# Rotary embedding of a two-block network: the exchange of feature pairs by transfers inside SBUF instead of products on TensorE

## The reference

```python
def apply_rope(x, cos, sin):
    ...
    a, b, c_, d = jnp.split(x, 4, axis=-1)
    rot = jnp.concatenate([-b, a, -d, c_], -1)
    return (x * cos + rot * sin).astype(x.dtype)
```

## Time and profile before

| | us |
|---|---|
| median of three runs | 1642.85 |
| lowest, highest | 1642.05, 1642.93 |
| span of the profiled execution (first to last instruction) | 1641.9 |
| TensorE busy in it | 1581.9 (96%) |
| VectorE busy | 828.0 (50%) |
| ScalarE busy | 735.2 (45%) |
| GpSimd busy | 0.9 |

### The profile page before, as it was taken

The page is one execution under the profiler, slowest core; times in us unless marked ns, Lnnn a source line. Parts: engine busy times, 40 slices in busy tenths (PEclk is TensorE's granted clock), DMA queues, the critical chain, the costliest instruction groups (busy, mean ns, idle before and its releaser), DMA issues.

```text
span 1641.9 us, 27059 instructions
## 1 busy us (share of the span) xinstructions
PE 1581.9 (96%) x11296; PEld 1223.5 (75%) x11296; DVE 828.0 (50%) x1461; ACT 735.2 (45%) x1140; POOL 0.9 (0%) x5
## 2 busy tenths in 40 slices
PE   8999989999999999999989999999999999999987
PEld 5646567777787778789858999998988788535443
DVE  2536664644434444543575756665677675212223
ACT  3545552633212332443463744546545542554444
POOL 0000000000000000000000000000000000000000
PEclk9999999999999999999999999999999999999999
DMA  9412632244334442422212446452442237799995
GB/s 390 157 39 82 212 118 103 103 181 178 124 120 154 166 162 96 180 77 103 78 36 94 158 151 218 148 174 107 163 143 99 82 131 314 298 407 420 421 421 205
DMA packets 43133, 287.91 MB, mean 175 GB/s; under 512 B 4848, under 2 KB 6000, under 8 KB 12160
## 3 DMA queue, kind: packets, MB, share of 16 engines
q1 hardware_dynamic: 42832, 285.99, 46.4%
q10 hardware_dynamic: 144, 0.06, 0.0%
q0 software_dynamic: 32, 0.07, 0.0%
HBM read 285.05 MB, written 1.05 MB: 174 GB/s over the span
## 4 chain that ended last, share of the span: by engine, by line
PE 82%; DVE 7%; ACT 5%; DMA 4%; issue 1%; SPq 0%; DVEq 0%; ACTq 0%
PE ps L539 17%; PE ps L541 16%; PE ps L540 16%; PE ps L2966 7%; DMA deep<-wts 4%; PE ps L590 2%; DVE WL L524 2%; PE ps L2826 1%; PE ps L1569 1%; PE ps L1540 1%; PE ps L1471 1%; PE ps L708 1%; PE ps L1648 1%; PE ps L1647 1%; PE ps L1646 1%
## 5 line engine op out<-in xcount | busy, mean ns | idle before, releaser
L539 PE MATMUL ps<-HH,WH 128*128 128x512 f32 (+2 forms) x1424 | 470.9, 331 | 10.1 <-DVE WL L524 5.7
L541 PE MATMUL ps<-HH,WL 128*128 128x512 f32 (+2 forms) x1424 | 459.9, 323 | 0.0
L540 PE MATMUL ps<-HL,WH 128*128 128x512 f32 (+2 forms) x1424 | 459.4, 323 | 0.0
L524 DVE TENSOR_TENSOR WL<-ring,WH 128x2048 fp32r<-128x2048 f32 (+2 forms) x134 | 281.5, 2103 | 143.5 <-ACT WH L514 143.4
L539 PEld LDWEIGHTS ps<-HH,WH 128*128 128x128 f32 x1424 | 270.0, 190 | 54.7 <-issue 22.5
L514 ACT ACTIVATE WH<-ring 128x2048 fp32r<-128x2048 f32 (+2 forms) x134 | 236.0, 1763 | 153.2 <-PE ps L541 76.6
L541 PEld LDWEIGHTS ps<-HH,WL 128*128 128x128 f32 x1424 | 270.0, 190 | 20.4
L540 PEld LDWEIGHTS ps<-HL,WH 128*128 128x128 f32 x1424 | 270.4, 190 | 18.4
L2966 PE MATMUL ps<-deep,arena 128*32 128x512 f32 (+1 forms) x872 | 114.4, 593 | 10.7 <-ACT late_x L2952 5.6
L539 PE MATMUL ps<-parts,WH 128*128 128x512 f32 (+1 forms) x352 | 119.9, 341 | 0.0
L540 PE MATMUL ps<-parts,WH 128*128 128x512 f32 (+1 forms) x352 | 118.4, 336 | 0.0
(11 more groups left out here) (401 smaller groups left out, 2185.3 us busy)
## 6 DMA issues: line engine op xcount, KB each, us to landing
ring<-wts SPq DMA_DIRECT2D x138, 1024.0 KB, 4.9
deep<-wts SPq DMA_DIRECT2D x92, 1024.0 KB, 16.3
ring<-wts SPq DMA_DIRECT2D x32, 704.0 KB, 4.0
arena<-wts SPq DMA_DIRECT2D x8, 1024.0 KB, 15.6
ring<-wts SPq DMA_DIRECT2D x4, 672.0 KB, 13.7
X<-xin SPq DMA_DIRECT2D x4, 512.0 KB, 16.5
ahead<-wts SPq DMA_DIRECT2D x2, 1024.0 KB, 8.5
deep<-wts SPq DMA_DIRECT2D x4, 512.0 KB, 20.5
```

The source lines that it names most:

```text
L524: e.tensor_tensor(lo, raw(i), hi.bitcast(F32), ALU.subtract).then_inc(*up("low", i))
L539: e.matmul(o, w[0][:, cols], x[0], start=k == 0, stop=False)
L540: e.matmul(o, w[0][:, cols], x[1], start=False, stop=False)
L541: return e.matmul(o, w[1][:, cols], x[0], start=False, stop=k == nk - 1)
```

## The change

The features of each rotated part are put in another order when the weights are laid out on the host (`paired`): the two features of a pair become neighbours, in rows 2i and 2i+1. Scores are sums over the features, and query and key are permuted alike, so that they stay the same. The sine table takes the sign (`rope_sign`). With that order the exchange of partners is an exchange of neighbouring rows. It is done by two transfers of 64 rows (16 for the 32-feature parts) of 1 KB each, from the tile to the temporary inside SBUF, issued from GpSimd's queue (`pool_rope`); the odd rows go to the even ones, and the even to the odd. GpSimd waits for the copy ("kept") and, from the third rope on, for the end of rope n-2, and then issues both; VectorE waits for both (semaphores `s_turned`, one for each temporary). VectorE's three operations stay; those on 96 rows now take only the 32 rows that turn. All of `pe_rope`'s products and their banks go, and with them the waits of TensorE for the copies (`pe_query_rope`, `pe_window_rope`, `pe_key_rope`, `query_rope`). Some marks are renamed, so that they share semaphores (`vs_tokens` into `vm.window`, `queries` into `keys.queries`, `query_tile` into `key_tile.query`, `vm_tile` into `key_tile.values`).

```diff
+def rope_order(dim):
     q = dim // 4
+    return [b + s * q + i for b in (0, 2 * q) for i in range(q) for s in range(2)]
+def paired(w, dim):
+    return w.reshape(w.shape[0], -1, dim)[:, :, rope_order(dim)].reshape(w.shape)
+def rope_sign(dim):
+    return np.where(np.arange(dim) // (dim // 4) % 2, 1, -1).astype(np.float32)[:, None]
...
     c64, s64 = rope_table(64)
+    c64, s64 = paired_rows(c64), paired_rows(s64 * rope_sign(64))
...
+        s_turned = [sem(f"s_turned{i}") for i in range(2)]
...
-        def pe_rope(e, key, dst, rows, perm):
-            b = bank(e, "rope", *key)
-            e.matmul(ps[0:rows, b, 0:256], C(perm, rows)[0:rows, :], dst[0:rows, 0:256], start=True,
-                     stop=True).then_inc(*up("turned", *key))
-            banks.give(b, "rope.sin", *key)
-
-        def dve_rope(e, key, dst, rows, cos, sin, TMP):
-            tm = TMP[0:rows, len(turned_keys) % 2, 0:256]
-            e.wait_ge(*at("turned", *key))
-            if len(turned_keys) >= 2:
+        def rope_place(rows, TMP):
+            low = 0 if rows == 128 else 64
+            return low, TMP[low:rows, len(turned_keys) % 2, 0:256]
+
+        def pool_rope(e, key, dst, rows, TMP, ready):
+            n = len(turned_keys)
+            low, tm = rope_place(rows, TMP)
+            e.wait_ge(*ready)
+            if n >= 2:
                 e.wait_ge(*at("rope", *turned_keys[-2]))
             turned_keys.append(key)
-            e.tensor_tensor(tm, B("rope", *key)[0:rows, 0:256], C(sin)[0:rows, :],
-                            ALU.mult).then_inc(*up("rope.sin", *key))
+            of = dst[low:rows, 0:256]
+            for x in range(2):
+                e.dma_start(tm[x:rows - low:2], of[1 - x:rows - low:2]).then_inc(s_turned[n % 2], 16)
+
+        def dve_rope(e, key, dst, rows, cos, sin, TMP):
+            n = len(turned_keys)
+            low, tm = rope_place(rows, TMP)
+            turned_keys.append(key)
+            e.wait_ge(s_turned[n % 2], 32 * (n // 2 + 1))
+            e.tensor_tensor(tm, tm, C(sin)[low:rows, :], ALU.mult).then_inc(*up("rope.sin", *key))
...
+        def pool_heads(e):
+            pool_rope(e, ("kept.ks",), KS, 128, TMPA, at("kept.ks"))
+            pool_rope(e, ("kept.kr",), KR, 96, TMPA, at("kept.kr"))
+            for h in range(2):
+                pool_query_rope(e, h)
+            for i in range(len(UNITS)):
+                if i in ROPED_AT:
+                    pool_query_rope(e, ROPED_AT[i])
+                if i in WINDOW_ROPED_AT:
+                    m = WINDOW_ROPED_AT[i]
+                    pool_rope(e, ("kept.qs", m), QS[:, m, :], 128, TMPA, at("kept.qs", m))
+
+        def pool_diff_inputs(e):
+            for name, t in (("kept.kd", Kd), ("kept.qd", Qd)):
+                for h in range(8):
+                    pool_rope(e, (name, h), t[:, h, :], 128, TMPD, at(name, h))
...
                     pe_tiles(e, c, ((128 * m, 128, "kept.kd", h),), m == 1)
-                    for r in ((0, 1), (2, 3), (4, 5), (6,))[h - 4]:
-                        pe_key_rope(e, r)
-            pe_key_rope(e, 7)
...
-                    pe_tiles(e, c, ((128 * m, 128, "kept.qd", h),), m == 1, 256, (lambda: query_rope(6)) if h == 7 else None)
-                    if 0 < h < 7:
-                        query_rope(h - 1)
+                    pe_tiles(e, c, ((128 * m, 128, "kept.qd", h),), m == 1, 256)
...
             pe_diff_turn(e, 0)
-            query_rope(7)
             pe_diff_scores(e, 2)
...
         def pool_program(e):
             e.dma_start(MT[:, :], meta).then_inc(s_m, 16)
+            pool_heads(e)
+            pool_diff_inputs(e)
```

More of the change, by code:

```diff
@@ L79, in rope_table, with paired_rows @@
     return cos.T.astype(np.float32), sin.T.astype(np.float32)
-def rope_perm(dim):
+def rope_order(dim):
     q = dim // 4
[L84 to L89, removed]
+    return [b + s * q + i for b in (0, 2 * q) for i in range(q) for s in range(2)]
+def paired(w, dim):
+    return w.reshape(w.shape[0], -1, dim)[:, :, rope_order(dim)].reshape(w.shape)
+def paired_rows(t):
+    return t[rope_order(len(t))]
+def rope_sign(dim):
+    return np.where(np.arange(dim) // (dim // 4) % 2, 1, -1).astype(np.float32)[:, None]
 def consts():
@@ L120, in consts @@
     c32, s32 = rope_table(32)
+    c32, s32 = paired_rows(c32), paired_rows(s32 * rope_sign(32))
     put("cos96", np.concatenate([np.ones((64, S), np.float32), c32]))
@@ L217, in host_chunk @@
         w = x["ab_w_in"][0][256 * key[1]:256 * key[1] + 256]
-        return pack_k(np.concatenate([w[:, :256], w[:, 768:]], 1))
+        return pack_k(np.concatenate([w[:, :256], w[:, 768:896], paired(w[:, 896:928], 32), paired(w[:, 928:1056], 64),
+                                      w[:, 1056:]], 1))
     if kind == "abq":
-        qs = x["ab_w_in"][0][:, 256:768].reshape(D, 8, 64)[:, QPERM].reshape(D, 512)
+        qs = paired(x["ab_w_in"][0][:, 256:768], 64).reshape(D, 8, 64)[:, QPERM].reshape(D, 512)
         return pack_k(qs[:, 256 * key[1]:256 * key[1] + 256])
     if kind == "qb":
-        return pack_k(x["mla_w_qb"][0][:, 384 * key[1]:384 * key[1] + 384])
+        w = x["mla_w_qb"][0][:, 384 * key[1]:384 * key[1] + 384].reshape(256, 4, 96)
+        turned = paired(w[:, :, 64:].reshape(256, 128), 32).reshape(256, 4, 32)
+        return pack_k(np.concatenate([w[:, :, :64], turned], 2).reshape(256, 384))
     if kind == "kvb":
@@ L239, in host_chunk @@
     if kind == "din":
-        return pack_k(x["diff_w_in"][0][:, 256 * key[1]:256 * key[1] + 256])
+        w = x["diff_w_in"][0][:, 256 * key[1]:256 * key[1] + 256]
+        return pack_k(paired(w, 64) if key[1] < 8 else w)
     if kind == "dout":
@@ L1067, in dve_rope @@
             e.wait_ge(*at("rope.cos", *key))
-            e.tensor_tensor(dst[0:rows, 0:256], dst[0:rows, 0:256], tm, ALU.add).then_inc(*up("rope", *key))
+            e.tensor_tensor(dst[low:rows, 0:256], dst[low:rows, 0:256], tm, ALU.add).then_inc(*up("rope", *key))
         HP = parts(8, 512)
@@ L1155, in pe_inputs @@
             t.then_inc(*up("turned.vs"))
[L1156 to L1160, removed]
+            banks.give(b, "vm.window")
             pe_mod(e, 0, 10)
@@ L1168, in pe_inputs, with pe_tiles @@
             pe_tiles(e, c[1], ((128, 128, "kept.qs", 3),))
-        def pe_tiles(e, c, tiles, ends=True, n=512, halfway=None):
+        def pe_tiles(e, c, tiles, ends=True, n=512):
             w = weights(e, c)
@@ L1254, in act_inputs @@
             e.wait_ge(*at("turned.vs"))
-            e.activation(VS, B("turned.vs").rearrange("p (c m) -> p c m", c=4), ACT.Copy).then_inc(*up("vs_tokens"))
+            e.activation(VS, B("turned.vs").rearrange("p (c m) -> p c m", c=4), ACT.Copy).then_inc(*up("vm.window"))
             act_keep(e, QS[:, 2, :], 128, ("kept.qs", 2), at("tile", "kept.qs", 2))
@@ L1308, in pe_queries @@
         def pe_queries(e, w, i, h):
-            b = bank(e, "queries", h)
+            b = bank(e, "keys.queries", h)
             for k in range(2):
@@ L1312, in pe_queries, with pool_query_rope @@
                              stop=k == 1)
[L1313 to L1318, removed]
+            t.then_inc(*up("key_tile.query", h))
+            banks.give(b, "keys.queries", h)
+        def pool_query_rope(e, h):
+            pool_rope(e, ("qm", h), QM[:, h % 4, :], 96, TMPA, at("keys.queries", h))
         def act_queries(e, h):
-            e.wait_ge(*at("query_tile", h))
-            e.activation(QM[0:96, h % 4, :], B("queries", h)[0:96, :], ACT.Copy).then_inc(*up("queries", h))
+            e.wait_ge(*at("key_tile.query", h))
+            e.activation(QM[0:96, h % 4, :], B("keys.queries", h)[0:96, :], ACT.Copy).then_inc(*up("keys.queries", h))
         def dve_queries(e, h):
@@ L1341, in act_prepare @@
             act_keys(e, h)
-        def pe_window_rope(e, m):
-            e.wait_ge(*at("kept.qs", m))
-            pe_rope(e, ("kept.qs", m), QS[:, m, :], 128, "r128")
+        def pool_heads(e):
[13 more added lines that the diff above has]
+                    pool_rope(e, (name, h), t[:, h, :], 128, TMPD, at(name, h))
         def pe_heads(e):
             w = weights(e, index["kvb", 0])
-            for h in range(2):
-                pe_query_rope(e, h)
             for k in range(4):
@@ L1353, in pe_heads @@
                 e.matmul(ps[:, b, :], KV[:, 128 * k:128 * k + 128], w[:, 256:768], start=True,
-                         stop=True).then_inc(*up("vm_tile", k))
+                         stop=True).then_inc(*up("key_tile.values", k))
                 banks.give(b, "vm", k)
@@ L1374, in act_heads @@
             for k in range(4):
-                e.wait_ge(*at("vm_tile", k))
+                e.wait_ge(*at("key_tile.values", k))
                 e.activation(VM[:, k, :], B("vm", k), ACT.Copy).then_inc(*up("vm", k))
@@ L3334, in build @@
         offs = np.cumsum([0] + [128 * c for _, c in plan])
-        whole_free = {("kvb", 0): ("key_tile", 3), ("qb", 0): ("query_tile", 3), ("qb", 1): ("query_tile", 7),
```

(3 more changed lines are left out.)

22 lines of the change are left out of this document (2 added, 20 removed).

## The result

The changed kernel takes 1647.09 us in the median of 20 runs (1642.36 to 1649.91) against 1643.05 us of the kernel before (20 runs, 1641.98 to 1647.11): a ratio of 1.0023, 95% interval 1.0017 to 1.0030. The forecast was 1634.8, and the time lies outside its range. The profiled execution of the changed kernel took 1649.35 us, 2.3 above its median, with a span of 1647.5; before, the span was 1641.9.

The account below looks back on a forecast made before the run. PE, with 82% of the chain, was taken as the bound, VectorE as the limit at the second block's queries. Gains of 3.7, 3.9 and 0.4 us made 8.0 off 1642.85: 1634.8 us, range 1631.5 to 1644.5.

Parts of the forecast that it names:

- The keys' term: Second block's eight key ropes: all 3.9 us of product time on the chain goes, at every L in the bounds.
- KS, KR and the first two queries: First stretch: transfers here are covered by other work, so 2 x 0.87 us is gained.
- the prediction's own term: First stretch (KS, KR, eight MLA queries, four window queries): 3.7 us gained at L = 4, 4.7 at 3.
- L: Time from the end of ScalarE's copy to the landing of both transfers: between 2.9 and 6.5 us, taken as 4.0.
- The queries of the second block: Eight Qd ropes, where VectorE decides: 0.4 us gained of 3.4 at L = 4, 1.7 gained at L = 3.
- the sum: Whole kernel: gains of 3.7, 3.9 and 0.4 make 8.0 us at L = 4, 10.3 at L = 3.
- the first term: First stretch again: 4.5 us less the loss at query 3; 2.4 us gained was given for L = 5.
- a median landing of more than 5 us: Sign named for the forecast being wrong, read from how long the rope transfers take to land.
- the shares of 0.54 and 0.51: DMA engines half busy at some transfer moments, taken to make an L of less than 3 unlikely.
- Slower: Qd ropes at 805 to 822 us wait on two temporaries if weight loads delay transfers: 1646.4 at L = 6.5; chance 0.14.
- Starved splits: VectorE's splits hold up GpSimd's descriptors, rope 2's pair lands 1.8 us later, some 1 us lost: 1635.8; chance 0.04.
- All back: Nearly all product time returns because transfers land in 3 us or less: 1632.5 us; chance 0.17.

Follow-up runs that it names:

- e1: Changed kernel with SyncE's four loads that replace the query and key weights held until the ropes of query 3 and query 7 end: 1636.69 us.
- e3: Changed kernel with the heads' loads and the two 1 MB loads of the second block held together: 1634.74 us, 1635.82 when run again.
- e4: Changed kernel, loads in place, with 20 idle products on PE ahead of its waits for the ropes of query 3 and query 7: 1642.92 us.
- e6: Kernel before, with only the eight ropes of the second block's keys done by transfers, the others still by products: 1641.65 us.

## Why the prediction was wrong

**What was right.** The page and the chain had the bound right, and the terms came out where nothing disturbed them. The table gives the length of the stretches in the profiles, in us, cut at the first copy of MLA's values, the last product of the heads' turn, the first copy of the second block's values, and the first product that weighs its outputs:

| kernel | up to the values | heads | up to the second block's values | its queries and heads | rest |
|---|---|---|---|---|---|
| before | 97.7 | 136.3 | 512.1 | 119.4 | 776.4 |
| after | 94.6 | 144.2 | 508.0 | 123.2 | 777.5 |
| e1, heads' loads held | 96.2 | 134.9 | 508.0 | 121.5 | 778.3 |
| e3, all held | 94.3 | 134.9 | 508.1 | 116.9 | 779.1 |
| e4, PE kept busy | 96.4 | 139.7 | 508.1 | 119.8 | 778.2 |
| e6, keys alone | 97.2 | 136.2 | 508.0 | 121.0 | 778.4 |

The keys' term (3.9 us) measured 4.0 to 4.1 in every kernel that has the transfers there, and PE is busy 40.00 us of 40 between 700 and 740. KS, KR and the first two queries (1.7 us) lie in the first column, which moves by 1 to 2 us with the arrival of the input; in the profile of the changed kernel 1.35 of its 3.1 us are there before any rope. The heads with their loads held take 1.4 us less, and in both profiles a dip of the clock that the kernel before does not have is in that (0.63 at 112 to 116 in e1; 0.86 and 0.72 at 220 to 228 in e3). From the first of the heads' exponentials to the last, ahead of the dip in e3, it takes 121.3 us (99.5 to 220.8) against 124.2 before (103.0 to 227.2): 2.9 less, and the prediction's own term has 3.0 at L = 3 (4.7 less the 1.7 of the first column). The queries of the second block take up to 2.5 less (1.7 at L = 3).

That the sum, 8.0, lies between the gains of the two runs with the loads held, 8.4 and 7.1, is luck. It was worked out for an L of 4; at the quiet L of 2.6 that is measured below, the prediction's sum is over 10.3 (hence the 1632.5 expected of e3), and these runs stay 2 to 3 us under that. The dips of the clock seen in these profiles are likely a part of it; how large a part, no run shows. (At L = 5 the first term should read 4.5 - 1.8 = 2.7 and not 2.4; nothing hangs on it.) The rest differs by 1 to 3 us among the profiles, for which no run shows a cause in the change.

**Where it failed: one L for all ropes.** The step is "L lies between 2.9 and 6.5. I take ... 4.0". From the end of a copy to the landing of both transfers it took 2.6 us in quiet (rope 0 of Qd: 790.40 to 792.97), below the lower bound, and 5.8, 6.6 and 6.2 at query 3, query 7 and rope 2 (106.42 to 112.18, 146.77 to 153.41, 796.17 to 802.37), once above the upper bound. L had two values and not one, and the larger fell on three ropes that had less room than that: at query 3 the scores start at 113.82, where a quiet L of 2.5 would have given 106.42 + 2.5 + 1.63 = 110.55: 3.3 us, ahead of any cost of the clock. The sign named for this, "a median landing of more than 5 us", did not show: the medians are 1.6 us (16 KB) and 1.8 (64 KB). A few late transfers at places with no room were enough. The row that gives the lower bound was itself a load, and the shares of 0.54 and 0.51 are means over a load and a pause: in slices of 2 us the trace of before has 0.69 at 110, 0.92 at 112 and 0.15 at 114. The question to ask of the earlier trace rows was which instruction sets the load free; it was the one that fed the rope.

**And the clock, which the sum did not hold.** The sum counts a stand of PE at its length and has no term for the clock. The half clock behind it costs 3.4 us more at query 3 and 2.7 at query 7 in the profile, and 4.2 us for both by the run that keeps PE busy.

**The rivals.** "Slower" named the loads as the condition and came out on the right side (1646.4 against 1647.1), but its chain did not run, so that the nearness is luck: through the ropes of Qd every idle time of GpSimd is ended by ScalarE's copy (70.5 us [<-ACT X L1195], the whole), none by the rope before last. "Starved splits" fell: the pair issued at 804.32, under VectorE's split of 803.58 to 805.86, cost GpSimd 1.06 us and landed in 1.8, like its neighbours. On that the Trainium skill ("SBUF — State Buffer", section "Who interferes with whom"), where a two-operand operation of VectorE did not stall such transfers, agrees with the trace. "All back" had the quiet L right; the estimate of 2.15 us for a landing by the Trainium skill ("DMA: Bandwidth & Descriptors", section "Anatomy of one DMA — SWDGE (gpsimd) path") was close to the measured 1.8.

What a load in front does can be set beside a rule of the Trainium skill ("DMA: Bandwidth & Descriptors", section "Queues, rings and completion order"): each DMA engine takes the queues in turn, a whole packet of some 9 to 17 descriptors at a time. The trace counts a megabyte as 128 pieces of 8 KB, 8 for each engine. If such a piece is a descriptor, an engine's whole part of a load fits into one turn, and a pair that comes behind it waits for all of it, as measured; had the queues changed after every piece, a pair would hardly be delayed. No run here shows the size of a turn.

**Not tried.** A wait of SyncE for the landing of a pair instead of for the end of its rope, and another place for the preparation of queries 3 and 7, were not run.

## What to carry to other kernels

A small transfer that someone waits for must be looked at together with the large one that is set free at the same moment: ask what the producing instruction was the last user of, and let the large load wait for a mark behind the small transfer where it has time. Price a new stand of PE with the half clock behind it, and look whether idle products into a bank that is about to be overwritten can bridge it. A mean DMA share of one half is no estimate of the delay at an instant; the spread of landings beside and without a load is.

## What the runs showed of the hardware

- A transfer of 16 to 64 KB inside SBUF from GpSimd's queue costs GpSimd 0.52 to 0.53 us and lands 1.6 to 1.8 us after its issue in quiet; 3.5 to 3.6 with 512 KB just ahead of it, 4.8 to 6.4 with 1 MB or more. On ScalarE's queue a pair took 3.5 to 6.3 at the same places: of one pair, the transfer 0.3 us ahead of a load 1.8, the one 0.3 us behind it 5.3.
- PE's granted clock fell to 0.50 after stands of 4.77 and 3.49 us (query 3 of the changed kernel and with half a load) and of 2.12 us (query 7 of the changed kernel), not after 0.34. With the loads held PE stood for about 2 us at query 3, and there both happened. PE in order of time, the first line from e3, the second from its repetition, the third from e1:

```profile
110.61 1.96 PE L1488 MATMUL ps<-arena 96*128 96x512 f32 x4 [1.89 <-DVE arena L1085]
```

```profile
112.22 3.61 PE L1488 MATMUL ps<-arena 96*128 96x512 f32 x4 [1.98 <-DVE arena L1085]
```

```profile
112.48 3.17 PE L1488 MATMUL ps<-arena 96*128 96x512 f32 x4 [1.89 <-DVE arena L1085]
```

The scores took 1.96 us after 1.89 us of standing, 3.61 after 1.98, and 3.17 after the same 1.89 in e1. So the length of the stand alone does not decide; what tips it was not settled.
